# State-space steps in a hybrid encoder block: decay exponents from broadcast running sums instead of products on TensorE

## The chip, the cores and the metric

The kernel runs on one core of a Trainium2 chip. The metric is the device time of one execution in microseconds (us). Engines are called TensorE (PE in the profile), VectorE (DVE), ScalarE (ACT), GpSimd (POOL) and SyncE (SP); each works through its own queue in order. SyncE's queue issues most of the DMA transfers.

## The reference, cut to what matters

One encoder layer on 512 tokens: an input projection, a state-space branch (Mamba-2 style, both directions), an S5 branch, a mix with a layer norm, and a mixture of 16 experts. All in float32. The change lies in the state-space branch, whose scan per direction is

```
xdt = xh * dt
cs = cumsum(dt * a)                       # within a chunk of 128 tokens
seg = cs[q] - cs[s]
decay = where(q >= s, exp(seg), 0)
cb = einsum('qgn,sgn->qsg', cc, bc)
wts = cb[..., None] * decay
y_diag = einsum('qsgh,sghp->qghp', wts, xdt)
y_off = einsum('qgn,ghpn->qghp', cc, prev) * exp(cs)
y = y_f + y_b + xh * d_skip               # forward scan, backward scan, skip
y = y * silu(z)                           # then a grouped RMS norm and w_out
```

There are 24 heads of 64 in 4 groups of 6, and 4 chunks of 128 tokens. Both exponents of the two directions are sums of negative numbers, and for a pair of tokens only one direction applies.

## The kernel before

The program is one block with a hand-written instruction stream for each engine, ordered by semaphores. In order of time: transposes of x and parameters; the S5 branch with the gate projections filling TensorE (from some 90 to 330 us); projection, convolution and transposes of the state-space inputs (to 427); the state-space steps (to about 630); the mix of both branches and the output projection (to about 850); the experts, whose weights (554 MB) stream through a ring of buffers until the end.

The state-space stage has 16 steps i, one for each group g and chunk c (i = 4g + c). For a step:

- GpSimd makes two arrays of 768 columns, `rhs_f` and `rhs_b` (L592, L593): a triangular mask times the log decay of each of the six heads. For a new group it first makes `bc_prod` (L589).
- TensorE (`scores_and_segments`, two steps ahead) makes the scores of 128 x 128 and a column of diagonal scores in PSUM bank 4, and with four products of 384 columns (`m_gt` by `rhs_f`, `m_lt` by `rhs_b`, accumulated) the exponents of both directions in banks 2 and 3.
- ScalarE (`decays`) takes exp of them from PSUM into `emat`. It also makes `dmat` from the step sizes (six operations), copies the transposed result of the last step, squares and takes a root for the norm, and puts SiLU on a z tile. The functions need three table loads a step.
- VectorE (`mixing_matrix`) forms the diagonal factor `diag_x` (L1752), and multiplies `emat` by the scores (L1754, reads PSUM) and by `dmat` (L1756) into `gmat`.
- TensorE (`y_products`) multiplies the states by C into banks 6 and 7 (one or two products of 384 columns) and the six heads' `gmat` by x into bank 5 (six products of 64 columns).
- VectorE sums y: L1783 (x times `diag_x`), L1786 and L1788 (the terms of banks 6 and 7 times their decay, into SBUF), L1791 (adds), L1792 (adds bank 5, signals `y_read`), L1795 (times SiLU of z, signals `gate_ready`).
- Then `mixing_matrix(i + 2)`, `carry` (L1737, L1739 or L1742) for the next group's states, `normalized(i)` (L1761, L1764) and `weighted_x` (L1726).

TensorE's order in a step is: `y_products(i)`, `scores_and_segments(i + 2)`, `y_transposed(i - 1)` (L1183), then for the first three chunks of the first three groups a wait for `y_read` of this step and `added_states` (two products of 384 columns for the next group, into banks 6 and 7), then a z tile (`z_tile(i + 2)`, eight products of 384 columns).

All plain products are issued by one helper (L947) and all of ScalarE's activations by another (L612).

Of the kernel before, what the change touches and what calls it, by code (L numbers as in the profile page):

```python
# [41 lines left out]
T = 4  # L42
# [120 lines left out]
def encoder(nc, A, out):  # L163
# [18 lines left out]
    g_dram = nc.dram_tensor("gate_scratch", (4, P, TT, 512), F32, kind="Internal").ap()  # L182
    toep_dram = nc.dram_tensor("toeplitz_scratch", (S5_W, (2 * T - 1) * S5_K), F32, kind="Internal").ap()

    with ExitStack() as ctx:
# [11 lines left out]
        m_le, m_gt, m_ge, m_lt, ones = (C.take(P) for _ in range(5))  # L197
        chunk_no = C.take(NC)
        conv_w, conv_b = C.take(XBC // P, CONV), C.take(XBC // P)
        dt_bias, a_neg = C.take(2 * HEADS), C.take(2 * HEADS)  # L200
        dt_step, diag_x = C.take(TT, HEADS), C.take(2, HG)
# [76 lines left out]
        rhs_f, rhs_b = S.take(HG, P), S.take(HG, P)  # L278
        bc_prod = S.take(SEQ)

# [50 lines left out]
        xw_ready st_ps carried cb_ps segm_ps segm_exp mats_ready dmat_ready bc_ready g_ready yd_ps y_read gate_ready rms_sqrt  # L331
# [8 lines left out]
        slice_loaded = [sem(f"slice_loaded_{i}") for i in range(NW)]  # L340
        unit_loaded = [sem(f"unit_loaded_{i}") for i in range(LANDINGS)]
# [25 lines left out]
        def _(sp):  # L367
# [68 lines left out]
            slices(FIRST_XBC + 2, FIRST_MIX + 1)  # L436

            sp.wait_ge(s.gate_ready, (GROUPS - 1) * TT)
            sp.wait_ge(s.y5_stored, 16 * 2 * T * NQ)
# [65 lines left out]
        def _(pool):  # L505
# [102 lines left out]
        def _(act):  # L608
# [1369 lines left out]
```

## Time and profile before

| | |
|---|---|
| median of 3 runs | 2182.41 us (2177.91 to 2184.29) |
| profiled execution | 2182.37 us |
| its span | 2180.5 us |
| mean granted TensorE clock | 0.952 |
| busy: TensorE, VectorE, ScalarE, GpSimd | 1980.1, 601.0, 381.4, 217.7 us |
| DMA | 625.47 MB, mean 287 GB/s |

The profiled execution is the one that the rows come from. The clock column says which share of full speed (2.4 GHz) TensorE was granted: 1.00 is 2.4 GHz, 0.50 is 1.2 GHz. A matrix product in float32 shows as two MATMUL records. PEld are weight loads, which overlap the products. "idle before" is the idle time of an engine just ahead of an instruction, with what released it.

### The profile page before, as it was taken

To read this page: it belongs to the slowest core of one execution; us is meant where nothing else is said; L and a number is where in the kernel's file an instruction comes from. 1 tells how busy PE (TensorE), PEld (TensorE's weight loads), DVE (VectorE), ACT (ScalarE), POOL (GpSimd) and SP (SyncE) were. 2 spreads that over 40 slices of the span, in tenths; PEclk is the share of its full clock that TensorE was granted. 3 is DMA by queue.
4 is the path that set the end of the run, shared out by engine and by line. 5 is a ranking of instruction groups with operands and counts; after the bars stand their busy time and mean duration, and the time that the engine had idled before them with its cause. 6 is when DMAs were issued, how large, how long until landed. Compare 5 with 4: busy or idle time off the path is not lost.

```text
span 2180.5 us, 19987 instructions
## 1 busy us (share of the span) xinstructions
PE 1980.1 (91%) x8382; PEld 938.9 (43%) x8382; DVE 601.0 (28%) x1101; ACT 381.4 (17%) x684; POOL 217.7 (10%) x238
## 2 busy tenths in 40 slices
PE   8989999999989999799988988988988988988887
PEld 4646554456654445434333333334333333333332
DVE  6598756487731115200100100100100100100102
ACT  1334312267740002010000000000000000000001
POOL 1776400022200000000000000000000000000001
PEclk9899999999989999899999999999989999999999
DMA  5622312100104245899999999999999999999995
GB/s 142 126 71 76 112 42 86 58 29 30 58 29 164 69 169 249 356 423 424 428 427 428 428 427 426 428 427 427 428 426 427 428 426 426 429 426 427 428 426 214
DMA packets 88073, 625.47 MB, mean 287 GB/s; under 512 B 21180, under 2 KB 34736, under 8 KB 57776
## 3 DMA queue, kind: packets, MB, share of 16 engines
q1 hardware_dynamic: 75552, 616.41, 68.9%
q10 hardware_dynamic: 12432, 7.79, 1.2%
q8 instruction: 66, 1.08, 0.2%
q14 instruction: 23, 0.19, 0.0%
HBM read 614.39 MB, written 9.78 MB: 286 GB/s over the span
## 4 chain that ended last, share of the span: by engine, by line
PE 60%; DMA 28%; DVE 3%; ACT 2%; issue 1%; POOL 1%; SPq 0%; DVEq 0%; POOLq 0%
PE ps L947 59%; DMA arena<-in_w_e 28%; ACT arena L612 1%; PE ps L1062 0%; DVE arena L1863 0%; DVE arena L1861 0%; DVE arena L1791 0%; DVE arena L1954 0%; DVE arena L1911 0%; ACT L612 0%; POOL arena L492 0%; PE ps L1432 0%; PE ps L1122 0%; DVE arena L1752 0%; DVE arena L1948 0%
## 5 line engine op out<-in xcount | busy, mean ns | idle before, releaser
L947 PE MATMUL ps<-arena 128*64 128x512 f32 (+6 forms) x7850 | 1915.3, 528 | 168.8 <-DMA arena<-in_w_e 107.5
L947 PEld LDWEIGHTS ps<-arena 128*64 128x64 f32 (+2 forms) x7850 | 876.1, 163 | 1183.0 <-issue 1044.5
L612 ACT ACTIVATE arena<-ps 128x512 f32<-128x512 f32 (+5 forms) x292 | 164.8, 595 | 1661.8 <-PE ps L947 954.5
L1920 DVE TENSOR_TENSOR arena<-arena,ps 128x512 f32<-128x512 f32 (+1 forms) x48 | 30.2, 644 | 575.3 <-PE ps L947 575.3
L604 POOL TENSOR_TENSOR arena<-arena 128x1024 f32<-128x1024 f32 x3 | 7.1, 2355 | 1366.2 <-ACT arena L612 1366.2
L1929 DVE TENSOR_TENSOR arena<-arena,ps 128x512 f32<-128x512 f32 x48 | 33.1, 690 | 332.0 <-PE ps L947 332.0
L612 ACT ACTIVATE arena<-arena 128x128 f32<-128x128 f32 (+8 forms) x250 | 110.0, 503 | 82.9 <-DVE arena L1827 20.8
L612 ACT ACT_TABLE_LOAD x74 | 94.9, 1283 | 23.5 <-issue 21.8
L1711 DVE SCALAR_TENSOR_TENSOR arena<-arena 128x512 f32<-128x512 f32 x80 | 60.2, 753 | 2.8
L1911 DVE TENSOR_TENSOR arena<-arena 128x512 f32<-128x512 f32 x8 | 5.6, 694 | 181.9 <-PE ps L1432 181.8
L592 POOL TENSOR_TENSOR arena<-arena 128x768 f32<-128x768 f32 x16 | 24.4, 1524 | 101.2 <-PE ps L947 101.2
L1513 DVE TENSOR_TENSOR arena<-arena 128x320 f32<-128x320 f32 x48 | 28.6, 658 | 0.6
L1809 DVE TENSOR_TENSOR arena<-ps,arena 128x512 f32<-128x512 f32 x8 | 5.5, 691 | 74.8 <-PE ps L947 38.7
L492 POOL TENSOR_TENSOR arena<-arena 128x256 f32<-128x256 f32 x40 | 24.9, 656 | 8.1 <-ACT arena L612 7.4
L1817 DVE TENSOR_TENSOR arena<-ps,arena 128x512 f32<-128x512 f32 x8 | 5.5, 693 | 71.0 <-PE ps L947 71.0
L593 POOL TENSOR_TENSOR arena<-arena 128x768 f32<-128x768 f32 x16 | 24.9, 1554 | 0.0
L589 POOL TENSOR_TENSOR arena<-arena 128x512 f32<-128x512 f32 x4 | 5.6, 1402 | 180.6 <-ACT arena L612 159.9
L1398 PE MATMUL ps<-arena 128*128 128x128 f32 x176 | 23.4, 289 | 0.0
L1398 PEld LDWEIGHTS ps<-arena 128*128 128x128 f32 x176 | 21.8, 210 | 3.1 <-DVE arena L1920 3.1
L1708 DVE TENSOR_SCALAR arena<-arena 128x512 f32<-128x512 f32 x20 | 10.9, 546 | 38.1 <-ACT arena L612 38.1
L529 POOL TENSOR_TENSOR arena<-arena 128x512 f32<-128x512 f32 (+4 forms) x19 | 16.9, 888 | 44.8 <-DVE arena L1517 26.9
L1931 DVE SCALAR_TENSOR_TENSOR arena<-arena,ps 128x512 f32<-128x512 f32 x8 | 5.5, 690 | 54.9 <-PE ps L947 54.9
(192 smaller groups left out, 679.8 us busy)
## 6 DMA issues: line engine op xcount, KB each, us to landing
arena<-in_w_e SPq DMA_DIRECT2D x120, 2816.0 KB, 29.3
arena<-in_w_e SPq DMA_DIRECT2D x80, 2048.0 KB, 27.7
arena<-in_w_e SPq DMA_DIRECT2D x16, 1408.0 KB, 22.0
arena<-in_w_in SPq DMA_DIRECT2D x9, 2048.0 KB, 8.4
arena<-in_w_e SPq DMA_DIRECT2D x16, 1024.0 KB, 30.6
arena<-in_w_in SPq DMA_DIRECT2D x5, 1536.0 KB, 6.4
arena<-in_w_out_ssd SPq DMA_DIRECT2D x4, 1536.0 KB, 6.7
gate_scratch<-arena ACTq DMA_DIRECT2D x16, 256.0 KB, 2.4
```

The source lines that it names most:

```text
L492: n.done(eng.tensor_tensor(tmp[t], x, y, ALU.mult))
L529: n.done(pool.tensor_tensor(out[0], x[0], y[0], ALU.mult))
L592: pool.tensor_tensor(rhs_f, first(m_le, HG), last(da[:, c, f], P), ALU.mult)
L593: pool.tensor_tensor(rhs_b, first(m_ge, HG), last(da[:, c, b], P), ALU.mult).then_inc(s.mats_ready, 1)
L612: return act.activation(out, in_, func, **kw)
L947: return pe.matmul(out, lhsT, rhs, start=a, stop=z)
L1398: r = pe.transpose(ps[:, i, P * t:P * t + P], block[:, t, :], ident)
L1513: n.done(tt(tv[t], x, y, ALU.mult))
L1708: r = ts(cacc[:, j], raw[:, j, 0:SEQ], conv_w[:, i, 0:1], conv_b[:, i:i + 1], ALU.mult, ALU.add)
L1711: r = stt(cacc[:, j], raw[:, j, k:k + SEQ], conv_w[:, i, k:k + 1], cacc[:, j], ALU.mult, ALU.add)
L1920: tt(o, o, ps[:, i, 0:w], ALU.mult).then_inc(s.hid_ready, 1)
L1929: r = tt(o, o, ps[:, 6 + k % 2, :], ALU.add)
```

## The change

The running sums of the log decays are already computed once for all steps (`m_le` and `m_ge` by `da`, PSUM bank 5). They are now also kept as they are: ScalarE copies them into `cum` (in the place of two masks that are no longer needed), TensorE transposes them (two transposes), ScalarE copies the result to SBUF and stores it in a DRAM scratch of 96 rows of 128 for each direction.

In the state-space stage, SyncE loads for each step the six rows of both directions, broadcast to all 128 partitions (2 x 768 columns, 768 KB), into one of two buffers. GpSimd subtracts the own token's sums from them (two operations of 768 columns, `diff_f` and `diff_b`, in place of the two mask products). VectorE takes the smaller of the two (`decay_exponents`, one operation of 768 columns, three steps ahead), and ScalarE takes exp in place. The four TensorE products of a step are gone. Both directions' differences are right where they are negative, and the smaller of the two is the one that applies.

Also changed:
- The scores alternate between banks 4 and 2. The four diagonal score columns of a group are made at once, and `diag_x` with two operations for a group instead of one for each step.
- The terms of banks 6 and 7 are multiplied by their decay in place in PSUM, and the last sum is written to bank 5. The semaphore `y_read` is gone: TensorE waits for `gate_ready`, one VectorE operation later, wherever it waited for `y_read`.
- Three of the weight slices are issued between the row loads, and the load of S5's result stands behind them.

```diff
+    cum_dram = nc.dram_tensor("cumulative_scratch", (2, TT * HEADS, P), F32, kind="Internal").ap()
...
         m_le, m_gt, m_ge, m_lt, ones = (C.take(P) for _ in range(5))
+        cum = arena[:, C.at - 3 * P:C.at - 3 * P + 2 * TT * HEADS].rearrange("p (d c h) -> p d c h", d=2, c=TT)
         chunk_no = C.take(NC)
         conv_w, conv_b = C.take(XBC // P, CONV), C.take(XBC // P)
         dt_bias, a_neg = C.take(2 * HEADS), C.take(2 * HEADS)
-        dt_step, diag_x = C.take(TT, HEADS), C.take(2, HG)
+        dt_step, diag_x = C.take(TT, HEADS), C.take(2, TT, HG)
...
-        rhs_f, rhs_b = S.take(HG, P), S.take(HG, P)
+        diff_f, diff_b = S.take(HG, P), S.take(HG, P)
         bc_prod = S.take(SEQ)
+        cum_rows = S.take(2, 2, HG, P)
...
-            slices(FIRST_XBC + 2, FIRST_MIX + 1)
+            slices(FIRST_XBC + 2, FIRST_Z + 2)
+            sp.wait_ge(s.y5_stored, 16 * 2 * T * NQ)
+            sp.wait_ge(s.g_stored, 16 * GATES)
+            sp.wait_ge(s.cum_stored, 16)
+            for i in range(GROUPS * TT):
+                g, c = divmod(i, TT)
+                if i >= 2:
+                    sp.wait_ge(s.diff_ready, i - 1)
+                rows = cum_dram[:, HEADS * c + HG * g:HEADS * c + HG * g + HG, :].rearrange("d h q -> d (h q)")
+                sp.dma_start(cum_rows[:, i % 2].rearrange("p d h q -> p d (h q)"), rows.partition_broadcast(P)).then_inc(cum_loaded[i % 2], 16)
+                if i in (6, 10, 14):
+                    slices(FIRST_Z + 2 + (i - 6) // 4, FIRST_Z + 3 + (i - 6) // 4)
...
@@ -581,16 +596,17 @@
             pool.wait_ge(s.nat_ps, 12)
             for i in range(GROUPS * TT):
                 g, c = divmod(i, TT)
-                f, b = slice(HG * g, HG * g + HG), slice(HEADS + HG * g, HEADS + HG * g + HG)
                 if c == 0:
                     pool.wait_ge(s.silu_done, 17 + g)
                     if g >= 1:
-                        pool.wait_ge(s.cb_ps, i)
+                        pool.wait_ge(s.cb_ps, i - TT + 1)
                     pool.tensor_tensor(bc_prod, bT[:, g, :], cT[:, g, :], ALU.mult).then_inc(s.bc_ready, 1)
+                pool.wait_ge(cum_loaded[i % 2], 16 * (i // 2 + 1))
                 if i >= 1:
-                    pool.wait_ge(s.segm_ps, i)
-                pool.tensor_tensor(rhs_f, first(m_le, HG), last(da[:, c, f], P), ALU.mult)
-                pool.tensor_tensor(rhs_b, first(m_ge, HG), last(da[:, c, b], P), ALU.mult).then_inc(s.mats_ready, 1)
+                    pool.wait_ge(s.diff_min, i)
+                h = slice(HG * g, HG * g + HG)
+                pool.tensor_tensor(diff_f, cum_rows[:, i % 2, 0], last(cum[:, 0, c, h], P), ALU.subtract)
+                pool.tensor_tensor(diff_b, cum_rows[:, i % 2, 1], last(cum[:, 1, c, h], P), ALU.subtract).then_inc(s.diff_ready, 1)
...
             f(w_end[:, :, 0:H], seg[:, 2], ACT.Exp)
             f(w_end[:, :, H:2 * H], seg[:, 3], ACT.Exp)
+            f(cum.rearrange("p d c h -> p (d c h)"), ps[:, 5, 0:8 * H], ACT.Copy)
             f(e_all, ps[:, 6, 0:8 * H].rearrange("p (c h) -> p c h", c=TT), ACT.Exp).then_inc(s.seg_exp, 1)
+            act.wait_ge(s.seg_ps, 2)
+            f(y5[0:TT * H, 0:2 * P], ps[0:TT * H, 3, 0:2 * P], ACT.Copy).then_inc(s.seg_exp, 1)
+            act.wait_ge(s.seg_exp, 2)
+            act.dma_start(cum_dram.rearrange("d r q -> r d q"), y5[0:TT * H, 0:2 * P].rearrange("r (d q) -> r d q", d=2)).then_inc(s.cum_stored, 16)
             def gelu(q):
                 act.wait_ge(s.y5_ps, q + 1)
-                if q >= 1:
+                if q == 0:
+                    act.wait_ge(s.cum_stored, 16)
+                else:
                     act.wait_ge(s.y5_stored, 16 * 2 * T * q)
                 f(y5, ps[:, 7, :], ACT.Gelu_apprx_tanh).then_inc(s.y5_copied, 1)
...
             def decays(i):
-                act.wait_ge(s.segm_ps, i + 1)
-                if i >= 1:
-                    act.wait_ge(s.g_ready, i)
-                f(emat.rearrange("p (a b) q -> p a (b q)", a=2), ps[:, 2:4, 0:GI], ACT.Exp).then_inc(s.segm_exp, 1)
+                act.wait_ge(s.diff_min, i + 1)
...
-                n.link(f(ty[:, 0], ty[:, 3], ACT.Square, accum_out=rms[:, i % 2, 0:1]))
+                n.link(f(ty[:, 1], ty[:, 3], ACT.Square, accum_out=rms[:, i % 2, 0:1]))
...
             mm(ps[:, 6, 0:8 * H].rearrange("p (c h) -> p c h", c=TT), ones, da, True, True).then_inc(s.seg_ps, 1)
+            pe.wait_ge(s.seg_exp, 1)
+            for d in range(2):
+                r = pe.transpose(ps[0:TT * H, 3, P * d:P * d + P], cum[:, d].rearrange("p c h -> p (c h)"), ident)
+            r.then_inc(s.seg_ps, 1)
...
                 pe.wait_ge(s.u_loaded, 16 * 2 * T)
+                if q == 0:
+                    pe.wait_ge(s.seg_exp, 2)
...
-            def scores_and_segments(i):
+            def scores(i):
                 g, c = divmod(i, TT)
+                if i >= 2:
+                    pe.wait_ge(s.g_ready, i - 1)
+                if c == 0:
+                    pe.wait_ge(s.bc_ready, g + 1)
+                    for k in range(TT):
+                        mm(ps[:, score_bank[0], P + k:P + k + 1], bc_prod[:, P * k:P * k + P], ones[:, 0:1], True, True)
                 q = slice(P * c, P * c + P)
-                if i >= 1:
-                    pe.wait_ge(s.g_ready, i)
-                pe.wait_ge(s.bc_ready, g + 1)
-                mm(ps[:, 4, P:P + 1], bc_prod[:, q], ones[:, 0:1], True, True)
-                mm(ps[:, 4, 0:P], bT[:, g, q], cT[:, g, q], True, True).then_inc(s.cb_ps, 1)
-                pe.wait_ge(s.mats_ready, i + 1)
-                if i >= 1:
-                    pe.wait_ge(s.segm_exp, i)
-                for a in range(2):
-                    o = ps[:, 2 + a, 0:GI].rearrange("p (h q) -> p h q", h=3)
-                    mm(o, m_gt, rhs_f[:, 3 * a:3 * a + 3, :], True, False)
-                    r = mm(o, m_lt, rhs_b[:, 3 * a:3 * a + 3, :], False, True)
-                r.then_inc(s.segm_ps, 1)
+                mm(ps[:, score_bank[i % 2], 0:P], bT[:, g, q], cT[:, g, q], True, True).then_inc(s.cb_ps, 1)
             def y_products(i):
...
                 pe.wait_ge(s.carried, 6 * (g + 1) + ahead)
                 if i >= 1:
-                    pe.wait_ge(s.y_read, i)
+                    pe.wait_ge(s.gate_ready, i)
                 if c >= 1:
...
                 if c < TT - 1:
...
             for j in range(TT - 1):
...
             for i in range(GROUPS * TT):
                 g, c = divmod(i, TT)
                 y_products(i)
                 if i + 2 < GROUPS * TT:
-                    scores_and_segments(i + 2)
+                    scores(i + 2)
                 if i >= 1:
                     y_transposed(i - 1)
                 if g + 1 < GROUPS and c < TT - 1:
-                    pe.wait_ge(s.y_read, i + 1)
+                    pe.wait_ge(s.gate_ready, i + 1)
                     added_states(g + 1, c)
                 if i + Z_AHEAD < GROUPS * TT:
                     if (i + Z_AHEAD) % TT == 0:
...
@@ -1741,17 +1762,24 @@
                         dve.wait_ge(s.st_ps, i + 1)
                         dve.tensor_copy(to, ps[:, 6 + d, 0:GI]).then_inc(s.carried, 1)
+            def decay_exponents(i):
+
+                dve.wait_ge(s.diff_ready, i + 1)
+                tt(emat, diff_f, diff_b, ALU.min).then_inc(s.diff_min, 1)
+
             def mixing_matrix(i):
+                g, c = divmod(i, TT)
+                dve.wait_ge(s.cb_ps, i + 1)
+                if c == 0:
+                    own = dtime[:, :, HEADS + HG * g:HEADS + HG * g + HG]
+                    n.link(tt(diag_x[:, g % 2], own, last(ps[:, score_bank[0], P:P + TT], HG), ALU.mult))
+                    n.done(tt(diag_x[:, g % 2], diag_x[:, g % 2], first(d_row[:, HG * g:HG * g + HG], TT), ALU.add))
                 dve.wait_ge(s.segm_exp, i + 1)
-                dve.wait_ge(s.cb_ps, i + 1)
                 if i >= 2:
                     dve.wait_ge(s.yd_ps, i - 1)
                 o = gmat[:, i % 2]
-                g, c = divmod(i, TT)
-                n.done(stt(diag_x[:, i % 2], dtime[:, c, HEADS + HG * g:HEADS + HG * g + HG], ps[:, 4, P:P + 1],
-                           d_row[:, HG * g:HG * g + HG], ALU.mult, ALU.add))
-                n.link(tt(o, emat, first(ps[:, 4, 0:P], HG), ALU.mult))
+                n.link(tt(o, emat, first(ps[:, score_bank[i % 2], 0:P], HG), ALU.mult))
                 dve.wait_ge(s.dmat_ready, i + 1)
                 tt(o, o, dmat[:, i % 2], ALU.mult).then_inc(s.g_ready, 1)
...
                 dve.wait_ge(s.yn_ready, i + 1)
+            decay_exponents(0)
             for j in range(TT - 1):
                 weighted_x(0, j)
                 if j == 1:
                     mixing_matrix(0)
+                    decay_exponents(1)
                 carry(0, j)
             mixing_matrix(1)
+            decay_exponents(2)
             for i in range(GROUPS * TT):
                 g, c = divmod(i, TT)
                 f, b = slice(HG * g, HG * g + HG), slice(HEADS + HG * g, HEADS + HG * g + HG)
...
-                y0, y1, y2 = ty[:, 0], ty[:, 1], ty[:, 2]
-                n.done(tt(h3(y0), h3(xs[:, c, gi]), bc(diag_x[:, i % 2]), ALU.mult))
+                y0, terms = ty[:, 0], []
+                n.done(tt(h3(y0), h3(xs[:, c, gi]), bc(diag_x[:, g % 2, c]), ALU.mult))
                 dve.wait_ge(s.yd_ps, i + 1)
                 if c >= 1:
-                    n.done(tt(h3(y1), h3(ps[:, 6, 0:GI]), bc(e_cs[:, c, f]), ALU.mult))
+                    terms.append(ps[:, 6, 0:GI])
+                    n.done(tt(h3(terms[-1]), h3(terms[-1]), bc(e_cs[:, c, f]), ALU.mult))
                 if c < TT - 1:
-                    n.done(tt(h3(y2), h3(ps[:, 7, 0:GI]), bc(e_cs[:, c, b]), ALU.mult))
+                    terms.append(ps[:, 7, 0:GI])
+                    n.done(tt(h3(terms[-1]), h3(terms[-1]), bc(e_cs[:, c, b]), ALU.mult))
                 n.wait()
-                for y in ([y1] if c >= 1 else []) + ([y2] if c < TT - 1 else []):
+                for y in terms:
                     n.link(tt(y0, y0, y, ALU.add))
-                tt(y0, y0, ps[:, 5, 0:GI], ALU.add).then_inc(s.y_read, 1)
-                dve.wait_ge(s.y_read, i + 1)
+                y = ps[:, 5, 0:GI]
+                n.link(tt(y, y, y0, ALU.add))
                 dve.wait_ge(s.z_silu, g * TT + c + 1)
-                tt(ty[:, 3], y0, zg[g % 2][:, c], ALU.mult).then_inc(s.gate_ready, 1)
+                tt(ty[:, 3], y, zg[g % 2][:, c], ALU.mult).then_inc(s.gate_ready, 1)
                 if i + 2 < GROUPS * TT:
                     mixing_matrix(i + 2)
+                if i + 3 < GROUPS * TT:
+                    decay_exponents(i + 3)
                 if more:
                     carry(g + 1, c)
             normalized(GROUPS * TT - 1)
```

## Rows read from the trace of the kernel before

**Rows 1.** The page: the chain that ended last, by engine, then by line.
```profile
PE 60%; DMA 28%; DVE 3%; ACT 2%; issue 1%; POOL 1%; SPq 0%; DVEq 0%; POOLq 0%
PE ps L947 59%; DMA arena<-in_w_e 28%; ACT arena L612 1%; PE ps L1062 0%; DVE arena L1863 0%; DVE arena L1861 0%; DVE arena L1791 0%; DVE arena L1954 0%; DVE arena L1911 0%; ACT L612 0%; POOL arena L492 0%; PE ps L1432 0%; PE ps L1122 0%; DVE arena L1752 0%; DVE arena L1948 0%
```

**Rows 2.** Busy time of each engine in one group of four steps.
```profile
482.80:530.80 48.00, 47.69 (x199) 30.94 (x197) 36.65 (x61) 36.25 (x68) 13.35 (x9) 1.00 0.10 34
```

**Rows 3.** Groups of instructions, 440 to 617 us: busy, mean ns | idle before.
```profile
L1756 DVE TENSOR_TENSOR arena<-arena 128x768 f32<-128x768 f32 x16 | 19.4, 1212 | 0.5
L1754 DVE TENSOR_TENSOR arena<-arena,ps 128x768 f32<-128x768 f32 x16 | 15.1, 944 | 0.0
...
L1752 DVE SCALAR_TENSOR_TENSOR arena<-arena,ps 128x6 f32<-128x6 f32 x16 | 12.8, 802 | 15.1 <-ACT arena L612 15.1
L612 ACT ACTIVATE arena<-ps 128x768 f32<-128x768 f32 x15 | 12.2, 813 | 43.1 <-PE ps L947 43.1
...
L1726 DVE TENSOR_TENSOR arena<-arena 128x384 f32<-128x384 f32 x21 | 10.8, 554 | 0.3
```

**Rows 4.** The chain in order of time: start, us, what.
```profile
483.13 11.46 PE ps L947 x46
494.60 0.33 PE ps L1183 x3
494.93 10.17 PE ps L947 x42
```

**Rows 5.** Timeline of one step: start, us, engine, line, operation.
```profile
479.76 0.56 DVE L1786 TENSOR_TENSOR arena<-ps,arena 128x384 f32<-128x384 f32 x1 [0.88 <-PE ps L947]
...
482.01 0.56 DVE L1792 TENSOR_TENSOR arena<-arena,ps 128x384 f32<-128x384 f32 x1
...
482.60 0.56 DVE L1795 TENSOR_TENSOR arena<-arena 128x384 f32<-128x384 f32 x1
...
482.89 1.60 POOL L592 TENSOR_TENSOR arena<-arena 128x768 f32<-128x768 f32 x1 [10.06 <-PE ps L947]
...
483.69 0.82 DVE L1752 SCALAR_TENSOR_TENSOR arena<-arena,ps 128x6 f32<-128x6 f32 x1 [0.53 <-ACT arena L612]
...
484.45 1.47 POOL L593 TENSOR_TENSOR arena<-arena 128x768 f32<-128x768 f32 x1
...
485.41 1.33 DVE L1756 TENSOR_TENSOR arena<-arena 128x768 f32<-128x768 f32 x1
```

**Rows 6.** Timeline: three later starts of a step's y sums.
```profile
502.06 0.56 DVE L1788 TENSOR_TENSOR arena<-ps,arena 128x384 f32<-128x384 f32 x1 [1.54 <-PE ps L947]
...
514.50 0.56 DVE L1786 TENSOR_TENSOR arena<-ps,arena 128x384 f32<-128x384 f32 x1 [2.60 <-PE ps L947]
...
527.77 0.56 DVE L1786 TENSOR_TENSOR arena<-ps,arena 128x384 f32<-128x384 f32 x1 [0.88 <-PE ps L947]
```

**Rows 7.** Timeline of the stage's start.
```profile
424.44 0.37 SPq L392 DMA_DIRECT2D arena<-in_w_in  x1
...
429.64 2.44 DVE L1726 TENSOR_TENSOR arena<-arena 128x384 f32<-128x384 f32 x2 [0.86 <-ACT arena L612]
429.87 1.79 POOL L592 TENSOR_TENSOR arena<-arena 128x768 f32<-128x768 f32 x1
...
442.79 0.49 ACT L612 ACTIVATE arena<-ps 128x384 f32<-128x384 f32 x1 [4.34 <-PE ps L947]
```

**Rows 8.** DMA issues: KB each, us from issue to landing.
```profile
arena<-in_w_in SPq DMA_DIRECT2D x5, 1536.0 KB, 6.4
...
arena<-in_ln_g SPq DMA_DIRECT2D x1, 512.0 KB, 13.1
```

**Rows 9.** Timeline of PE, expert stage: a wait and what follows it.
```profile
1111.02 11.38 PE L947 MATMUL ps<-arena 128*64 128x512 f32 x48 [2.07 <-DMA arena<-in_w_e]
```

**Rows 10.** Three us after a wait of 2.07, and of 1.32; granted clock third from the end.
```profile
1111.00:1114.00 3.00, 2.98 (x8) 1.12 (x10) 0.00 (x0) 0.00 (x0) 0.00 (x0) 0.57 0.97 413
...
1153.90:1156.90 3.00, 2.98 (x14) 1.25 (x16) 0.00 (x0) 0.00 (x0) 0.00 (x0) 1.00 1.02 431
```

More of the change, by code:

```diff
@@ L277, in encoder @@
         S = Space(arena, S2.at - 4 * SEQ, top)
-        rhs_f, rhs_b = S.take(HG, P), S.take(HG, P)
+        diff_f, diff_b = S.take(HG, P), S.take(HG, P)
         bc_prod = S.take(SEQ)
+        cum_rows = S.take(2, 2, HG, P)
+        score_bank = (4, 2)
         S = Space(arena, late_at, top)
@@ L330, in encoder @@
         pool_step m_cleared maps_cleared xbc_ps xbc_raw conv_done silu_done nat_ps nat_copied z_ps z_silu
-        xw_ready st_ps carried cb_ps segm_ps segm_exp mats_ready dmat_ready bc_ready g_ready yd_ps y_read gate_ready rms_sqrt
+        xw_ready st_ps carried cb_ps diff_min segm_exp diff_ready cum_stored dmat_ready bc_ready g_ready yd_ps gate_ready rms_sqrt
         yn_ready yt_ps yt_copied mix_ps mix_sig mix_read glu_done mix_ready mixT_ps mixT_copied wo_ps wo_read
@@ L340, in encoder @@
         slice_loaded = [sem(f"slice_loaded_{i}") for i in range(NW)]
+        cum_loaded = [sem(f"cum_loaded_{i}") for i in range(2)]
         unit_loaded = [sem(f"unit_loaded_{i}") for i in range(LANDINGS)]
@@ L435, in _ @@
             y_to_dram(NQ - 1)
-            slices(FIRST_XBC + 2, FIRST_MIX + 1)
+            slices(FIRST_XBC + 2, FIRST_Z + 2)
[10 more added lines that the diff above has]
+                    slices(FIRST_Z + 2 + (i - 6) // 4, FIRST_Z + 3 + (i - 6) // 4)
             sp.wait_ge(s.gate_ready, (GROUPS - 1) * TT)
-            sp.wait_ge(s.y5_stored, 16 * 2 * T * NQ)
             sp.dma_start(ty5, y_dram.rearrange("(n p) t c -> p n (t c)", p=P)).then_inc(s.yT5_loaded, 16)
@@ L791, in decays @@
             def decays(i):
-                act.wait_ge(s.segm_ps, i + 1)
-                if i >= 1:
-                    act.wait_ge(s.g_ready, i)
-                f(emat.rearrange("p (a b) q -> p a (b q)", a=2), ps[:, 2:4, 0:GI], ACT.Exp).then_inc(s.segm_exp, 1)
+                act.wait_ge(s.diff_min, i + 1)
+                f(emat, emat, ACT.Exp).then_inc(s.segm_exp, 1)
             def dt_matrix(i):
@@ L1192, in _ @@
             pe.wait_ge(s.nat_copied, 16)
-            scores_and_segments(0)
+            scores(0)
             pe.wait_ge(s.silu_done, 20)
@@ L1199, in _ @@
             pe.wait_ge(s.z_silu, 2)
-            scores_and_segments(1)
+            scores(1)
             for i in range(GROUPS * TT):
@@ L1226, in _ @@
                     pe.wait_ge(s.yt_copied, 3 * GROUPS * TT)
-                    pe.wait_ge(s.y_read, GROUPS * TT)
+                    pe.wait_ge(s.gate_ready, GROUPS * TT)
                 for half in range(halves):
```

## The prediction

> **What bounds the kernel now.** I read the chain that ended last first. It is 60% TensorE and 28% the expert weights' DMA [rows 1]: each microsecond that the part ahead of the experts gains or loses moves everything behind it. Then the busy times of one group of four steps in the stage that the change touches: 48.0 us, of which TensorE is busy 47.7, VectorE 36.7, ScalarE 36.3 and GpSimd 13.4 [rows 2]. So TensorE bounds this stage, and its next limits lie 11 us lower. The reader should see how tempting that is: the change takes four large products a step from the bounding engine. The question is what TensorE waits for when they are gone, and for that I read the chain in order of time [rows 4] and the timeline of a step [rows 5, 6].
>
> **The price of a product.** Between two sets of transposes TensorE issued 46 records in 11.46 us, and in the next step 42 in 10.17 [rows 4]. Four records are two 384-column products: 1.29 us, 0.645 each. So a z tile (eight) is 5.16, the exponents (four) 2.58, two added states 1.29. Of the 42 records, 26 are products (8.38 us), which leaves 1.79 for the scores and the six 64-column products: I put 0.33 on scores, 1.45 on the six. Transposes are 0.33 [rows 4].
>
> **Where TensorE's saving goes.** After a step's y products the old order is scores and exponents (0.33 + 2.58), transposes 0.33, and only then the wait for y_read, added states and z tile: 3.24 us of work while VectorE sums y. That sum took from 479.76 to 482.57, 2.81 us; the gate product ended at 483.16, at 3.40 [rows 5]. So now the wait costs nothing. After the change TensorE has 0.6 us of work there (scores, transposes), and the wait at the same place is for gate_ready, which comes at 3.4 in a step with both scan terms and at 2.3 in one with a single term (four VectorE operations of 0.58). The added states and the z tile stand behind this wait in TensorE's queue. In nine of the 16 steps (c = 0 to 2 of three groups) the 2.58 us become an idle wait of 1.7 to 2.8. Time from one y sum to the next, before [rows 5, 6] and after:
> - c 0 to 1: 12.4 before; after, 2.3 + 1.29 + 5.16 + y products 2.74 = 11.5.
> - c 1 to 2: 13.3 before (VectorE blocked behind GpSimd); after, 3.4 + 1.29 + 5.16 + 2.74 = 12.6.
> - c 2 to 3: 11.8 before; after, 3.4 + 1.29 + 5.16 + 2.1 = 12.0.
> - c 3 to 0: 10.5 before. TensorE has no such wait here and would need 7.9, but see the next part.
>
> **VectorE and GpSimd.** VectorE gains a min over 768 columns a step: L1756, the same form, takes 0.96 undisturbed. It loses L1752: 0.80 on average for six columns [rows 3]. That is no work but a block. GpSimd's L592 ran from 482.89 to 484.49; L1752 began at 483.69 and ended at 484.51. L1756 began at 485.41, GpSimd's L593 ended at 485.92, and L1756 took 1.33, ending 0.82 behind it [rows 5]. L1754, which reads PSUM, takes 0.94 beside the same GpSimd operations [rows 3]. So a VectorE operation with both inputs in SBUF stands still until GpSimd's ends. Now GpSimd starts when segm_ps comes, during the PSUM-reading product. After the change it starts when diff_min comes, that is at the end of the mixing, and its 2.95 us fall on carry, normalization, weighted x and the first y product, nearly all SBUF with SBUF. The y sums in PSUM escape it, which removes the block of c 1. In c 0 to 2 TensorE's 9 us between y sums cover the block. In c 3 they don't: VectorE has y sums 2.3, mixing 1.9, the two diagonal operations 0.4, min 0.9, and then one operation behind each of GpSimd's three (the two differences and the next group's bc_prod, some 4.3 us) with 0.4 to 0.5 of its own each: 10.3, where TensorE needs 7.9.
>
> The Trainium skill has this as a rule ("SBUF — State Buffer", the part on the two sides of SBUF): the port pair that VectorE and GpSimd share is an exclusive lock held for the whole instruction, and a VectorE operation with two SBUF inputs needs it. The trace agrees, with the 0.82 above; were there no lock, c 3 to 0 would be 7.9 and the whole below 2.4 us lower in each of two groups.
>
> **The sum of the steps.** Group 0: about -0.3 (its first interval was already 11.1). Group 1: 11.5 + 12.6 + 12.0 + 10.3 = 46.4 against 48.0, -1.6. Group 2: the same but its last interval, which leads into a group without weighted x, is 7.9: -4.0. Group 3 has no added states and so no wait: two intervals of 11.15 (3.24 + 5.16 + 2.74) fall to ScalarE's own 36.25 / 4 = 9.1 [rows 2]: -4.1. Together -10.0. ScalarE's exponentials cost what they did (0.81 from PSUM [rows 3]; the copy in SBUF some 0.05 more) and no longer wait.
>
> **The start.** Now weighted x starts at 429.64, and GpSimd's first product at 429.87, 5.4 us after the slice of z weights is issued at 424.44 [rows 7]. A 1,536 KB slice lands after 6.4 us [rows 8], so at 430.8. The first row pair (768 KB) is queued behind it: at most half of 6.4 more, at least perhaps 1.5. I take 433. Then differences 2.95, min 0.96: 436.8. VectorE's queue holds min ahead of the first weighted x, so this comes at 436.8 and its second half behind GpSimd's next difference, at 39.2. The z tile behind these states began about 437.6 (its SiLU at 442.79 [rows 7]) and now 39.9: 2.3 late. The further blocks by rows 2 and 3 of the exponents add about 1.7 until the first y sum: +4.0; bounds +1 (GpSimd hidden) and +7 (row at 436).
> Nothing else outside: the copy, two transposes and the store of the sums sit at 89 us beside GpSimd's own work, on which that stretch hangs; uncovered they would be 1.1. The three slices that now stand between row issues have four or more steps until use. The end (ScalarE's six copies of y5) is unchanged. So far: -10.0 + 4.0 = -6.0.
>
> **What the idle waits do to TensorE.** After a wait of 2.07 us, TensorE ran 8 records in 3.0 us with a granted clock of 0.57; after one of 1.32 us it ran 14, at 1.00 [rows 9, 10]. 0.57 is mostly the lower level, 1.2 of 2.4 GHz. I read the first three microseconds behind 14 waits of 1.95 to 2.73 us in the expert stage (as in rows 9): 13 show 8 to 10 records, one 14. Six records of some 0.21 us, and two more in the next three, are about 1.6 us for each such wait. In the stage now there is hardly a wait; the change puts a wait of 2.8, 2.4 or (c 0, where the block of c 3 delays y) about 4 us in each of nine steps, just ahead of added states and z tile, which are then on the path. Eight of nine, 1.6 each, is +13.1, and the start, where TensorE also waits, some +1.5. I take this: the row says it for waits of exactly this size. Sum: -6.0 + 14.6 = +8.6.
>
> The profiled execution took 2182.37 us (span 2180.5), the runs' median is 2182.41: I forecast 2191.0.
>
> **The rivals.**
> - The clock stays up (each wait's neighbours are long and dense, unlike the expert stage's; two waits of 1.6 and 1.9 us at the stage's start left no mark): -6.0, 2176.4. Chance 0.17. This is the one that ends on the other side: it decides if fewer than four of nine waits slow TensorE.
> - The lock does not bite (GpSimd's operations fall into VectorE's idle time) and the clock stays up: c 3 to 0 at 7.9 and a start 4 us earlier, about -15, 2167. Chance 0.06.
> - The full saving comes through, 16 x 2.58 = 41 less 16 x 0.05: 2142. It needs TensorE never to wait for y; the order of its queue speaks against it. Chance 0.03.
> - Longer low stretches: the waits of 4 us in c 0 and at the start cost 3.4 instead of 1.6, +6 on top: 2197. Chance 0.12.
> - The rows come late: a 512 KB broadcast behind other traffic landed after 13.1 us [rows 8], so 768 KB could take 20, against two buffers of 12 us each. If each row costs 1 us, 2207. Little other traffic here: chance 0.07.
> - Half of the waits slow it: about 2183. Chance 0.05.
> The forecast itself holds 0.50.
>
> **How the numbers follow.** No change is within 0.3%, 6.5 us, about what a measurement of this kernel can tell. The forecast case is 2191 with its own range 2186 to 2195; 70% of it lies above 2188.9. Slower: 0.35 + 0.12 + 0.07 + 0.01 = 0.55. Faster: half of the first rival, the next two: 0.17. The rest, 0.28, is no change. The range goes from the first rival (2175) to the long low stretches (2200).
>
> **What would show it.** TensorE's busy share in 435 to 630 falls, yet the stage keeps its length: the added states idle for the gate product nine times, 2.4 us and more; the granted clock in 450 to 600 falls from 1.00 to about 0.85; GpSimd's differences stand beside L1737, L1726 and L1783 with durations of 0.9 and more; intervals near 13.2, 14.2, 13.6, 10.3. Wrong if the clock stays at 1.00 (then 2176), if the first y sum is not later than 457, or if group 3 steps stay at 11.

## The result, and the profile after

The changed kernel takes 2197.53 us (median of 4 runs, 2196.18 to 2198.47) against 2182.39 of the kernel before on the same chip: a ratio of 1.0072 (95% interval 1.0054 to 1.0089). It is slower by 15 us, though four large products a step are gone from the engine that bounded the stage. The profiled spans differ by 15.1 us (2195.6 and 2180.5), and the account below is made on them.

The page of the changed kernel, the chain that ended last by engine (against [rows 1]) and the DMA issues (against [rows 8]):

```profile
PE 56%; DMA 31%; DVE 5%; ACT 2%; issue 1%; POOL 1%; SPq 0%; DVEq 0%
...
arena<-cumulative_scratch SPq DMA_DIRECT2D x16, 768.0 KB, 5.3
```

TensorE's share fell from 60% to 56% and VectorE's rose from 3% to 5%: the chain now changes over to VectorE inside the steps. Busy times of the stage's middle, in the order PE, PEld, DVE, ACT, POOL, then the granted clock:

```profile
450.00:500.00 50.00, 37.73 (x135) 23.90 (x134) 39.05 (x59) 28.67 (x55) 14.71 (x9) 0.83 0.33 101
500.00:550.00 50.00, 40.41 (x152) 26.05 (x151) 39.84 (x60) 36.39 (x67) 13.65 (x9) 0.83 0.25 82
550.00:600.00 50.00, 40.41 (x158) 26.46 (x157) 36.78 (x57) 32.45 (x60) 11.61 (x8) 0.88 0.28 91
```

In [rows 2] TensorE was busy 47.7 of 48.0 us at a clock of 1.00. Here it is busy 40.4 of 50, and slower while it is busy. What it waits for is in the waits of 430 to 650 us (total, times, longest), with the one wait for a transfer:

```profile
PE ps L968 <- DVE arena L1828: 33.8, 10, 6.5
...
POOL arena L608 <- DMA arena<-cumulative_scratch: 4.5, 1, 4.5
```

L1828 is the gate product. It takes 0.56 us, and each wait holds that much more than a wait for `y_read` would; no run puts the earlier signal back. TensorE's timeline over three steps shows those waits one by one, in brackets, ahead of the added states and the z tile:

```profile
514.33 12.12 PE L968 MATMUL ps<-arena 128*128 128x384 f32 x38 [4.70 <-DVE arena L1828]
526.29 0.49 PE L1204 MATMUL ps<-arena 128*128 128x128 f32 x3
529.68 12.15 PE L968 MATMUL ps<-arena 128*128 128x384 f32 x46 [2.90 <-DVE arena L1828]
541.67 0.49 PE L1204 MATMUL ps<-arena 128*128 128x128 f32 x3
544.16 11.92 PE L968 MATMUL ps<-arena 128*128 128x384 f32 x36 [2.00 <-DVE arena L1828]
555.92 0.49 PE L1204 MATMUL ps<-arena 128*128 128x128 f32 x3
```

The block of c = 2 was 46 records in 11.46 us in [rows 4]. Without the exponents it is 36 records, and yet it takes 11.92, with a wait of 2.00 on top. TensorE alone, cut into pieces (busy, then granted clock), shows why:

```profile
514.50:521.30 6.80, 6.80 (x14) 0.63 0.02 6
521.30:526.30 5.00, 5.00 (x27) 1.00 0.45 153
530.00:536.00 6.00, 6.00 (x15) 0.74 0.00 0
536.00:541.50 5.50, 5.50 (x32) 1.00 0.41 120
544.30:550.00 5.70, 5.70 (x9) 0.50 0.33 108
550.00:555.80 5.80, 5.80 (x27) 0.98 0.50 138
```

Behind each wait TensorE runs at the lower of its two levels (0.50, 1.2 GHz) and comes back later in the step: 14, 15 and 9 records where the second halves hold 27, 32 and 27.

The other side is VectorE beside GpSimd, at the end of a group (c = 3). First VectorE, then GpSimd:

```profile
505.50 0.95 DVE L1768 TENSOR_TENSOR arena<-arena 128x768 f32<-128x768 f32 x1
506.37 0.15 DVE L1789 RECIPROCAL arena<-arena 128x1 f32<-128x1 f32 x1
506.55 1.72 DVE L1792 TENSOR_SCALAR arena<-arena 128x384 f32<-128x384 f32 x1
508.31 3.24 DVE L1747 TENSOR_TENSOR arena<-arena 128x384 f32<-128x384 f32 x2
511.47 0.55 DVE L1814 TENSOR_TENSOR arena<-arena 128x384 f32<-128x384 f32 x1
```

```profile
506.59 1.47 POOL L608 TENSOR_TENSOR arena<-arena 128x768 f32<-128x768 f32 x1 [10.25 <-DVE arena L1768]
508.02 1.58 POOL L609 TENSOR_TENSOR arena<-arena 128x768 f32<-128x768 f32 x1
509.56 1.57 POOL L603 TENSOR_TENSOR arena<-arena 128x512 f32<-128x512 f32 x1
```

The min (L1768) releases the differences. The normalization (L1792) ends at 508.27, 0.2 behind L608; the two weighted x (L1747) take 3.24 instead of 1.1. Over the stage by form (busy, mean ns):

```profile
L1747 DVE TENSOR_TENSOR arena<-arena 128x384 f32<-128x384 f32 x24 | 22.7, 988 | 0.3
...
L1768 DVE TENSOR_TENSOR arena<-arena 128x768 f32<-128x768 f32 x16 | 15.3, 953 | 8.7 <-POOL arena L609 8.7
...
L1792 DVE TENSOR_SCALAR arena<-arena 128x384 f32<-128x384 f32 x16 | 14.3, 894 | 0.6
...
L1758 DVE TENSOR_TENSOR arena<-arena 128x384 f32<-128x384 f32 x16 | 13.5, 845 | 0.0
```

And the stage's start, against [rows 7]:

```profile
421.92 0.37 SPq L397 DMA_DIRECT2D arena<-in_w_in  x1
...
431.90 1.47 POOL L608 TENSOR_TENSOR arena<-arena 128x768 f32<-128x768 f32 x1 [4.50 <-DMA arena<-cumulative_scratch]
...
434.92 0.96 DVE L1768 TENSOR_TENSOR arena<-arena 128x768 f32<-128x768 f32 x1 [8.65 <-POOL arena L609]
...
436.49 1.62 PE L968 MATMUL ps<-arena 128*128 128x384 f32 x2 [5.94 <-DVE arena L1747]
```

The first rows come 4.5 us after GpSimd wants them; the differences, the min and weighted x follow in a chain, and TensorE waits 5.9 us at the end of it.

**The account.** Times from the start of one step's y sums to the next, in the second group (c 0 to 1, 1 to 2, 2 to 3, 3 to 0): before 12.4, 13.3, 11.8, 10.5; after 14.3, 14.5, 15.1, 10.6. From the first y sum to the last the 16 steps take 185.7 us (458.33 to 644.05), before 172.1 (455.36 to 627.44): +13.6. From the issue of the z slice to the first y sum, 36.4 (458.33 - 421.92) against 30.9 (455.36 - 424.44): +5.5. Ahead of that issue -2.5 (421.92 against 424.44), behind the last y sum -1.5 (1551.6 to the end of the span, before 1553.1). Sum +15.1.

### The profile page after: what moved, and what is told of

It is laid out like the page before. It is cut to its first block, busy times and chain, and to the rows that moved or that the text cites. A ratio compares the mean times of both kernels' runs of the same rounds, so it can differ in the third digit from the quotient of the medians.

```text
span 2195.6 us, 19736 instructions
## 1 busy us (share of the span) xinstructions
PE 1966.9 (90%) x8256; PEld 927.8 (42%) x8256; DVE 614.8 (28%) x1109; ACT 384.0 (17%) x686; POOL 220.4 (10%) x238
## 4 chain that ended last, share of the span: by engine, by line
PE 56%; DMA 31%; DVE 5%; ACT 2%; issue 1%; POOL 1%; SPq 0%; DVEq 0%
PE ps L968 55%; DMA arena<-in_w_e 31%; ACT arena L628 2%; ACT L628 1%; DVE arena L1824 1%; DVE arena L1747 0%; DMA arena<-cumulative_scratch 0%; DVE ps L1826 0%; PE ps L1089 0%; DVE arena L1898 0%; DVE arena L1896 0%; DVE arena L1828 0%; DVE ps L1818 0%; DVE arena L1989 0%; POOL arena L507 0%
## 5 line engine op out<-in xcount | busy, mean ns | idle before, releaser
L968 PE MATMUL ps<-arena 128*64 128x512 f32 (+8 forms) x7722 | 1901.6, 534 | 191.8 <-DMA arena<-in_w_e 100.4
L968 PEld LDWEIGHTS ps<-arena 128*64 128x64 f32 (+2 forms) x7722 | 867.1, 164 | 1207.9 <-issue 1068.1
L628 ACT ACTIVATE arena<-ps 128x512 f32<-128x512 f32 (+5 forms) x278 | 152.2, 580 | 1646.3 <-PE ps L968 936.5
L628 ACT ACTIVATE arena<-arena 128x128 f32<-128x128 f32 (+9 forms) x266 | 123.3, 523 | 105.8 <-DVE arena L1828 21.9
L608 POOL TENSOR_TENSOR arena<-arena 128x768 f32<-128x768 f32 x16 | 25.1, 1569 | 135.5 <-DVE arena L1768 131.0
L1747 DVE TENSOR_TENSOR arena<-arena 128x384 f32<-128x384 f32 x24 | 22.7, 988 | 0.3
L544 POOL TENSOR_TENSOR arena<-arena 128x512 f32<-128x512 f32 (+4 forms) x19 | 16.8, 886 | 45.9 <-DVE arena L1538 28.1
```

What stands on the lines that cost most here:

```text
L608: pool.tensor_tensor(diff_f, cum_rows[:, i % 2, 0], last(cum[:, 0, c, h], P), ALU.subtract)
L628: return act.activation(out, in_, func, **kw)
L968: return pe.matmul(out, lhsT, rhs, start=a, stop=z)
L1747: tt(h3(xw[:, d]), h3(xs[:, c, GI * g:GI * g + GI]), bc(w_end[:, c, h0:h0 + HG]), ALU.mult).then_inc(s.xw_ready, 1)
```

## The experiments

Each is the changed kernel with one edit, unless it says otherwise. The kernel before, beside them, had medians of 2181.2 to 2182.1. "Intervals" are the second group's times from y sum to y sum, as above.

**Is it the wait, or what the wait does to the clock?** Useless products fill the wait, so that TensorE does work there and the gate product comes no earlier:

```
+for k in range(4):          # e10: range(2)
+    mm(ps[:, 3, 0:GI], xT[:, 0, 0:P], xT[:, 1, 0:GI], True, True)
 pe.wait_ge(s.gate_ready, i + 1)
```

> The changed kernel, with four 384-column products of no use (x by x, into PSUM bank 3, which nobody reads) put back on TensorE ahead of its wait for gate_ready, in the nine steps with added states. Work is only added. If the fall of TensorE's clock after the idle waits carries the loss (the changed kernel shows 6.8 + 3.4 + 6.8 us at the lower level in each of three groups, half of which is lost: 25 us), the granted clock in 450 to 600 returns to 1.00, the steps from c 0 to 3 take 11.5, 12.6 and 12.0 us instead of 14.3, 14.5 and 15.1, and the time is about 2172 to 2177, below the kernel before. If instead VectorE and the lock with GpSimd set the steps, or the later semaphore does, the fillers change nothing or cost their own time: 2197 or more.

Measured 2180.02 (10 runs), 0.9993 (0.9984 to 1.0002): 17.5 us less than the changed kernel, from added work whose result nothing reads. TensorE's timeline:

```profile
510.32 9.57 PE L968 MATMUL ps<-arena 128*128 128x384 f32 x38 [2.13 <-DVE arena L1830]
519.73 0.49 PE L1204 MATMUL ps<-arena 128*128 128x128 f32 x3
520.06 2.75 PE L968 MATMUL ps<-arena 128*128 128x384 f32 x8
523.11 10.46 PE L968 MATMUL ps<-arena 128*128 128x384 f32 x46 [0.31 <-DVE arena L1830]
```

The 38 records that took 12.12 us now take 9.57, the 46 take 10.46 instead of 12.15. From the end of one to the start of the next there are still 3.2 us (519.89 to 523.11; after, 526.45 to 529.68): the step waits for VectorE as long as before, only TensorE doesn't lose speed by it. Intervals 11.7, 12.8, 12.5, 10.6. The run came 3 to 8 us above what was expected of it: low stretches remain in the first group (clock 0.93 in 450 to 500 us, behind a wait of 2.99 in c = 0), and in c = 2 the fillers themselves outlast the wait by 0.4.

> The changed kernel with two filler products ahead of the wait instead of four. The waits left are about 3.4 us in c 0, 1.5 in c 1 and 1.1 in c 2. If only waits of some 2 us or more bring the clock down, it falls once in a group instead of three times, the steps c 1 to 3 take 12.6 and 12.0 us as with four fillers, and the time is 2182 to 2188. If every wait counts alike in proportion to its length, it lies half way between 2197.5 and 2180: 2189; if the clock falls in all three, 2192 or more.

Measured 2184.68 (10 runs), 1.0016 (1.0006 to 1.0025):

```profile
509.89 12.49 PE L968 MATMUL ps<-arena 128*128 128x384 f32 x38 [3.41 <-DVE arena L1830]
...
525.61 10.46 PE L968 MATMUL ps<-arena 128*128 128x384 f32 x46 [1.60 <-DVE arena L1830]
...
538.40 8.93 PE L968 MATMUL ps<-arena 128*128 128x384 f32 x36 [0.71 <-DVE arena L1830]
```

The time lies where the first case had it. Intervals 14.6, 12.8, 12.1, 10.6. The waits of 1.60 and 0.71 leave the speed alone, in all three groups; that of 3.41 does not (12.49 for the 38 records, and 11.26 behind the same wait in the next group). With the four fillers' blocks these give the undisturbed durations of all three. Against them the changed kernel loses 12.12 - 9.57 = 2.55, 12.15 - 10.46 = 1.69 and 11.92 - 8.93 = 2.99 us, which is 7.2 in the second group. The same subtraction gives 6.4 in the first and 7.4 in the third: 21.0 together, 2.3 a wait.

**What the products had covered.** The kernel before, with its four exponent products left out (one product of a single column signals in their place):

```
-for a in range(2):
-    ...
-    mm(o, m_gt, rhs_f[...], True, False); r = mm(o, m_lt, rhs_b[...], False, True)
+mm(ps[:, 2, 0:1], m_gt, rhs_f[:, 0, 0:1], True, True).then_inc(s.segm_ps, 1)
```

> The kernel before, with the four exponent products of each step left out (one product of a single column signals in their place, so exp reads stale PSUM): 16 x 2.58 = 41 us of TensorE work less and nothing else changed, no broadcast rows, no min, GpSimd at its old place. If the idle wait and the clock are the cause, TensorE waits about 2.2 us for y_read in nine steps, the clock falls, these steps take 13.5 to 15 us, and the time is no better than before: 2180 to 2195. If the changed kernel's loss comes from its new work on VectorE, GpSimd and the DMA rows, this one gains in all steps that its other engines allow: 2160 or less.

Measured 2189.35 (5 runs), 1.0034 (1.0021 to 1.0047). Taking 41 us of products from the bounding engine, with no other edit, makes the old kernel slower:

```profile
508.78 9.91 PE L947 MATMUL ps<-arena 128*128 128x384 f32 x42 [0.83 <-DVE arena L1788]
...
522.80 11.94 PE L947 MATMUL ps<-arena 128*128 128x384 f32 x42 [3.72 <-DVE arena L1788]
```

42 records in 11.94 behind a wait, 9.91 behind a short one. Intervals 11.1, 16.0, 16.0, 8.1, where 13.5 to 15 was expected in three: the long waits stand in c = 1 and 2 (3.72 and 3.97), and in c = 0 of this group only 0.83 is left. In c = 1 and 2 they are longer than in the changed kernel (2.90 and 2.00), since GpSimd's products now start earlier and fall on the y sum: its two additions (VectorE, then GpSimd) take 2.98 instead of 1.1. So this run shows that the removed products turn into waits and a low clock without any of the new work; the size of its loss is partly GpSimd's.

```profile
519.17 2.98 DVE L1787 TENSOR_TENSOR arena<-arena 128x384 f32<-128x384 f32 x2
```

```profile
519.95 1.79 POOL L592 TENSOR_TENSOR arena<-arena 128x768 f32<-128x768 f32 x1
521.70 1.78 POOL L593 TENSOR_TENSOR arena<-arena 128x768 f32<-128x768 f32 x1
```

**Useful work in the wait.** The first four of the z tile's eight products move ahead of it:

```
+z_tile(*divmod(i + Z_AHEAD, TT), w, 0, 4)
 pe.wait_ge(s.gate_ready, i + 1)
 added_states(g + 1, c)
-z_tile(*divmod(i + Z_AHEAD, TT), w)
+z_tile(*divmod(i + Z_AHEAD, TT), w, 4)
```

> The changed kernel, with the first four of the z tile's eight products moved ahead of TensorE's wait for gate_ready (the same sum, the same bank). If TensorE's idle wait and the clock that falls with it are the loss, the clock returns to 1.00 and 2.6 us of each of the nine waits are used: steps near 10 to 10.5 us, bounded by VectorE and its blocks, and a time of about 2155 to 2163. If VectorE with the lock already sets the steps, the clock comes back but the steps stay at 12: about 2173.

Measured 2168.67 (4 runs), 0.9944 (0.9922 to 0.9965): 29 us below the changed kernel, 6 to 14 less gain than expected. Intervals 9.5, 11.9, 11.5, 10.6: the clock is back, but the steps lie between the two cases. In 500 to 550 us VectorE is now the busiest engine, 47.6 of 50:

```profile
500.00:550.00 50.00, 44.09 (x194) 28.94 (x193) 47.62 (x70) 42.15 (x78) 17.06 (x11) 1.00 0.34 111
```

The control is the same move in the kernel before, which has no idle wait there.

> The kernel before with the same move of half a z tile ahead of its wait for y_read. There TensorE has 3.24 us of work in a wait of 2.8, so it has nothing to fill: the time stays within 3 us of 2182. Only where VectorE's y sum was late behind GpSimd (0.7 us in c 1) can it gain. If the order itself were the gain of the half-tile version, this one would fall to 2170 too.

Measured 2181.37 (10 runs), 0.9999 (0.999 to 1.0008), as expected: the move is worth nothing where the exponents cover the wait.

**The lock.** GpSimd's differences are left out from the second step on; an operation of eight columns signals instead:

```
+pool.tensor_tensor(diff_f[:, 0, 0:8], cum_rows[..., 0:8], cum_rows[..., 0:8], ALU.subtract).then_inc(s.diff_ready, 1)
```

> The changed kernel, with GpSimd's two differences of 768 columns left out from the second step on (one operation of 8 columns signals in their place; the exponents are those of the first step). If the lock delays VectorE as the timeline reads, the interval from c 3 to c 0 falls from 10.5 to about 8 us, TensorE's wait in c 0 falls from 4.7 to 1.7 us so that the clock no longer falls there, and the time is about 2183 to 2187. The waits of c 1 and c 2 and their low clock stay. If the lock costs nothing, 2196 or more.

Measured 2188.33 (8 runs), 1.0025 (1.0015 to 1.0036), 1 to 5 us above what was expected. The interval of c 3 to 0 falls from 10.6 to 8.0. The clock's losses stay (18.7 us in nine steps, by the same subtraction), even behind the wait of c = 0, now 2.2, where none was expected:

```profile
514.05 11.25 PE L971 MATMUL ps<-arena 128*128 128x384 f32 x38 [2.17 <-DVE arena L1831]
...
528.52 13.43 PE L971 MATMUL ps<-arena 128*128 128x384 f32 x46 [2.89 <-DVE arena L1831]
```

> Half of the z tile ahead of the wait and GpSimd's differences left out, together. The half-tile version alone ran in 2168.7 with steps of 10.5 to 11.9 us and VectorE busy 95%. If VectorE's blocks behind GpSimd are the rest, steps fall to ScalarE's 9.3 to 9.8 and the time to about 2153 to 2158. If ScalarE or the row loads were the bound already, 2165 or more.

Both together: 2154.25 (4 runs), 0.9885 (0.9862 to 0.991). Half the z tile brought 29 us, the differences 9; together they bring 43. From the first y sum to the last the differences bring 10.3 us here (154.9 to 144.6) and 7.4 alone (185.7 to 178.4). The intervals are 10.1, 11.2, 10.8, 8.0: with half a z tile moved, VectorE bounds c 1 to 2 and 2 to 3 as well, and each falls by 0.7. The clock is 1.00 up to 550 us, as with the half tile alone; in the run without the differences alone it was 0.86 in 450 to 600.

**The start.** Row pairs 0 and 1 are loaded ahead of the last z slice instead of behind it:

```
-slices(FIRST_XBC + 2, FIRST_Z + 2)
+slices(FIRST_XBC + 2, FIRST_Z + 1)    # and the slice FIRST_Z + 1 where i == 2
```

> The changed kernel, with the first two row loads issued ahead of the last slice of z weights instead of behind it. In the changed kernel GpSimd waits 4.5 us for the first row. If the late row carries the late start (5.5 us from the stage's begin to the first y sum, against before), 3 to 5 us come back: about 2193. If the start is late because of VectorE's order and the blocks, under 1 us: 2197.

Measured 2192.22 (4 runs), 1.0049 (1.0033 to 1.0065). GpSimd's first difference starts at 428.70, right behind its first product, with no wait for the rows, and the first y sum at 454.4 instead of 458.3. The span is 4.0 shorter (2191.6). From the issue of the z slice to the first y sum it is now 31.1 us (423.27 to 454.4), 5.3 less than in the changed kernel and 0.2 more than before: nearly the whole late start hangs on the first rows.

**Where the min stands.** The min moves from the end of the mixing to just ahead of VectorE's wait for the y products, so that GpSimd's differences fall on the y sums, which have an operand in PSUM:

```
 n.done(tt(h3(y0), h3(xs[:, c, gi]), bc(diag_x[:, g % 2, c]), ALU.mult))
+if i + 2 < GROUPS * TT:
+    decay_exponents(i + 2)
 dve.wait_ge(s.yd_ps, i + 1)
 ...
-if i + 3 < GROUPS * TT:
-    decay_exponents(i + 3)
```

> The changed kernel with nothing but VectorE's min moved from behind the mixing to just ahead of its wait for the y products. GpSimd's differences then run beside the y sums in PSUM, so the lock should take nothing; TensorE's waits of c 1 and c 2 stay, and with them the low clock. The version without differences gained 9 us; this one should gain as much, 2186 to 2190, if the lock is what that one removed. If it had gained by something else (less of SBUF traffic or of the rows), this one stays at 2195 or more.

Measured 2185.03 (10 runs), 1.0018 (1.0008 to 1.0028): 12.5 us less than the changed kernel. VectorE's delays behind GpSimd are nearly gone, with GpSimd's work still there: weighted x takes 607 ns, the carry 557, the normalization 422, and c 3 to 0 falls to 7.7. In the second group the waits are 1.84, 2.89 and 2.00; behind the first the 38 records take 9.57, behind the other two 46 take 13.18 and 36 take 10.62. In the third group a wait of 1.84 stands in the same place, and the 38 records take 11.26. From the first y sum to the last the run gains 9.9 us (185.7 to 175.9), of which 4.2 are a smaller loss to the clock (16.8 instead of 21.0), and the start is 3.1 shorter.

> The changed kernel with half of the z tile ahead of the wait, the first two rows loaded ahead of the last z slice, and VectorE's min moved from behind the mixing to just ahead of its wait for the y products, so that GpSimd's differences fall beside the y sums, which read PSUM. If the lock bounds the half-tile version, its blocks (weighted x 0.99 us for 0.51, carry 0.85 for 0.55, normalization 0.89 for 0.42) go and the steps fall to 9.3 to 10: about 2153 to 2158. If the work of VectorE itself bounds it, only the early rows count: 2163 to 2165.

Half the z tile, the early rows and the late min together: 2145.87 (4 runs), 0.9838 (0.9823 to 0.9852). This is the best version, 36 us below the kernel before and 52 below the changed one. The windows, and VectorE's groups that had been blocked:

```profile
500.00:550.00 50.00, 48.64 (x217) 32.27 (x216) 45.27 (x83) 47.03 (x87) 15.47 (x12) 1.00 0.42 126
```

```profile
L1752 DVE TENSOR_TENSOR arena<-arena 128x384 f32<-128x384 f32 x24 | 13.6, 608 | 0.3
...
L1763 DVE TENSOR_TENSOR arena<-arena 128x384 f32<-128x384 f32 x16 | 10.1, 632 | 0.0
...
L1797 DVE TENSOR_SCALAR arena<-arena 128x384 f32<-128x384 f32 x16 | 6.8, 422 | 0.6
```

Weighted x takes 608 ns instead of 988, the carry 632 instead of 845, the normalization 422 instead of 894; TensorE is busy 48.6 of 50 us at a clock of 1.00. Intervals 10.5, 10.3, 10.0, 7.8. It came 7 us below what was expected.

## Why the prediction was right, and what it mis-sized

The direction and the mechanisms held; the forecast of +8.6 is 6.5 us short of the measured +15.1, and that is three misses which partly cancel: 7.9 too little for the clock in the steps, 2.6 too much gained in the steps without it, and 4.0 outside the stage the other way. The way the time went rests on the clock: less its 21.0 us, the changed kernel would stand near 2176.5 (an estimate), the first rival's time.

- **TensorE's saving becomes an idle wait: right.** Nine waits for the gate product, 4.7, 2.9 and 2.0 us in a group against the foreseen 4, 2.8, 2.4. The experiment without the exponent products shows it without the new work: 41 us of products gone, 7 us slower, with waits that GpSimd lengthens.
- **The steps without the clock: -10.0 foreseen, about -7.4.** Undisturbed intervals (c 0 to 1 and 1 to 2 of the four fillers, 2 to 3 of the two, 3 to 0 of the changed kernel) are 11.7, 12.8, 12.1, 10.6 against 11.5, 12.6, 12.0, 10.3 foreseen. Taken for the first group too they sum to 47.2, +0.5 against 46.7 before (foreseen -0.3). The second is -0.8 (-1.6), the third, whose last interval is 8.6 (7.9), -2.8 (-4.0), the last -4.3 (-4.1).
- **The lock: right.** c 3 to 0 is 10.6 and would be 8.0 without the differences; foreseen 10.3 and 7.9. What the working had too narrow is its condition, both inputs in SBUF: the normalization, a TENSOR_SCALAR with one input in SBUF, is blocked too, 894 ns against 422. The Trainium skill ("SBUF — State Buffer", the two sides of SBUF) gives the lock for two SBUF inputs and also for a VectorE operation in a 2-port mode. The trace agrees for the two inputs; whether the TENSOR_SCALAR ran in such a mode no trace here shows.
- **The start: right in size.** Foreseen +4.0 for the rows and the blocks and +1.5 for the clock, measured +5.5. With the rows early it is 31.1 us instead of 36.4, so 5.3 of the 5.5 hang on the first rows. How they divide between the blocks and the clock no run separates.
- **The cost of an idle wait: the term that was mis-sized.** "Eight of nine, 1.6 each, is +13.1" (eight times 1.6 is 12.8, so the sum stands 0.3 too high). By subtraction the clock cost 13.6 + 7.4 = 21.0 us in the steps, and the blocks say the same: 6.4, 7.2 and 7.4 in the three groups. That is 2.3 a wait, not 1.6, and all nine slowed. For the expert stage 1.6 had been read rightly, though only from the first three microseconds and an extension. The kernel before, from the wait of [rows 9] on until the pace is back:

```profile
1111.00:1114.00 3.00, 2.98 (x8) 1.12 (x10) 0.00 (x0) 0.00 (x0) 0.00 (x0) 0.57 0.97 413
1114.00:1117.00 3.00, 3.00 (x14) 1.17 (x12) 0.00 (x0) 0.00 (x0) 0.00 (x0) 0.86 1.02 426
1117.00:1120.00 3.00, 3.00 (x18) 1.37 (x16) 0.00 (x0) 0.00 (x0) 0.00 (x0) 1.00 1.00 428
```

  A clock of 0.57 and then 0.86 loses 3 x 0.43 + 3 x 0.14 = 1.7 us. The trace has 20 such waits of 1.95 to 2.73 us: 16 lose 1.5 to 1.7 us by the same sum, four lose nothing (the prediction had 13 of 14). What failed is that this price holds in the state-space stage as well. There the low stretch goes on for 5 us in c = 0 and for nearly 6 in c = 2 (9 records in 5.7 us at 0.50), and only c = 1 pays 1.7. Why it lasts longer than in the experts stays open. The chance of 0.12 for longer low stretches, priced 2197, held what came, though it gave them to the waits of 4 us alone, and the wait of 2.0 in c = 2 cost the most of the three.
- **The rivals.** The clock did not stay up (the 2176 case): with four fillers it nearly did, and the time was 2180, which is no change. That rows arrive late in every step did not happen: 5.3 us each, one wait of 4.5 in the stage. The full 41 us are out of reach in this order of TensorE's queue.
- **Outside the stage**, -2.5 ahead of it and -1.5 behind were not foreseen. Both lie within the scatter of single executions. The eight experiments that edit the changed kernel leave the code ahead of the stage and behind it as it is, and they issue that slice between 420.5 and 427.6 us and take 1550.2 to 1553.4 from the last y sum to the end. The gap of 15 us itself stands on the medians.

So +5.5 (start) - 7.4 + 21.0 (steps) - 2.5 - 1.5 = +15.1.

## What to carry to other kernels

Work taken from the bounding engine shortens the kernel only where something else can take its place in that engine's queue: look at which wait the removed work had covered, and move independent work ahead of it in the same edit (here four products of the z tile, worth 29 us). Price an idle wait of a TensorE that is on the path by what follows it, reading granted clock and records per microsecond until the pace is back, and give such a price a wide range when it comes from another stage: 1.7 us in the experts was 1.5 to 3.0 here. And where VectorE and GpSimd both work in SBUF, choose the instruction that releases GpSimd so that its work falls on VectorE's PSUM operations; moving one min was worth 12.5 us, blocks, start and clock together.

## What the hardware showed that I had not expected

- The length of a wait does not settle what it costs. A wait of 2.00 us in the changed kernel (c = 2) was followed by 5.7 us at 0.50; one of 2.13 behind four full products (four fillers) by none. Nor does the place in the program: in one execution with the late min, waits of 1.84 in c = 0 cost nothing in the second group and 1.7 us in the third (11.26 for 9.57), and with two fillers waits of 3.41 cost 2.9 and 1.7. 1.60 and 0.71 left no mark. What decides between them was not tried and stays open.
- Useless products made the kernel 17.5 us faster, though the step waits for VectorE as long as before: all of it is TensorE's pace behind the waits.
- VectorE's TENSOR_SCALAR, with one SBUF tensor as input, stood behind GpSimd's instruction up to 1.3 us (1.72 against 0.42).
- A broadcast of 768 KB from DRAM rows to 128 partitions lands 5.3 us after its issue, less than the 6.4 us of a 1,536 KB slice, and far from the 13.1 us of the 512 KB load in [rows 8] that I had put beside it.
